# SSD steps of a hybrid backbone: the forward products of the masked C.B scores move from GpSimd to ScalarE

## What is computed

```
def step(h, inp):                       # one chunk of 128 tokens
    cum = jnp.cumsum(dtc * a, axis=1)
    seg = cum[:, :, None, :] - cum[:, None, :, :]
    decay = jnp.exp(jnp.where(lower[None, :, :, None], seg, -jnp.inf))
    xdt = xc * dtc[..., None]
    scores = jnp.einsum('blhn,bshn->blsh', cc, bc) * decay
    y = jnp.einsum('blsh,bshp->blhp', scores, xdt)
    ...
yx_f, _ = _ssd_scan(xx, dtx[:, :, 0], a[0], bx, cx, sc_f)
yx_b, _ = _ssd_scan(flip(xx), flip(dtx[:, :, 1]), a[1], flip(bx), flip(cx), sc_b)
```

## Time and profile before

| | us |
|---|---|
| median of 3 runs | 1758.17 (1756.37 to 1759.17) |
| the profiled execution's own time | 1754.64 |
| its span | 1753.4 |
| TensorE busy | 1565.6 (89%) |
| VectorE busy | 1120.2 (64%) |
| ScalarE busy | 733.8 (42%) |
| GpSimd busy | 303.9 (17%) |

### The profile page before, as it was taken

How to read it: one execution, slowest core, us unless ns; L and a number is a source line. 1 busy time by engine, 2 the same in 40 slices (tenths; PEclk the granted TensorE clock), 3 DMA queues, 4 the chain that set the end, 5 groups by cost and what they waited for, 6 DMA issues and landing times.

```text
span 1753.4 us, 22888 instructions
## 1 busy us (share of the span) xinstructions
PE 1565.6 (89%) x8633; PEld 1283.8 (73%) x8633; DVE 1120.2 (64%) x1694; ACT 733.8 (42%) x1291; POOL 303.9 (17%) x379
## 2 busy tenths in 40 slices
PE   5699999999976999988878999989999899998877
PEld 2577877777765789766556877767788788887766
DVE  0257888887777465655645645535336778888875
ACT  1435444544434334355453522322334445554442
POOL 0011433343333101100000000000001023322330
PEclk7589999999978999999989989989899899999888
DMA  9432455335440322222432143442441343343333
GB/s 287 136 91 81 121 144 160 112 113 151 139 144 24 108 96 79 82 73 73 144 121 84 49 147 111 151 144 73 144 138 38 88 130 99 100 116 97 99 106 108
DMA packets 169422, 197.40 MB, mean 113 GB/s; under 512 B 9696, under 2 KB 151648, under 8 KB 169312
## 3 DMA queue, kind: packets, MB, share of 16 engines
q1 hardware_dynamic: 158480, 163.08, 29.2%
q0 software_dynamic: 9296, 30.19, 6.8%
q10 hardware_dynamic: 1536, 2.67, 0.5%
HBM read 194.59 MB, written 1.31 MB: 112 GB/s over the span
## 4 chain that ended last, share of the span: by engine, by line
PE 53%; DVE 28%; ACT 8%; issue 8%; DMA 2%; ACTq 0%; POOL 0%; DVEq 0%
PE ps L400 14%; PE ps L401 13%; PE ps L402 13%; DVE xc L809 6%; DVE w_lo L369 4%; PE ps L424 3%; DVE cum_b L817 3%; PE ps L562 2%; PE ps L568 2%; DMA raw<-in_mod_w 2%; ACT Wb L714 2%; DVE Wb L836 2%; DVE Hs L851 1%; ACT w_hi L362 1%; PE ps L1624 1%
## 5 line engine op out<-in xcount | busy, mean ns | idle before, releaser
L400 PE MATMUL ps<-h_hi,w_hi 128*128 128x512 f32 (+1 forms) x1056 | 407.1, 386 | 14.5 <-DVE w_lo L369 14.0
L401 PE MATMUL ps<-h_lo,w_hi 128*128 128x512 f32 (+1 forms) x1056 | 393.7, 373 | 0.0
L402 PE MATMUL ps<-h_hi,w_lo 128*128 128x512 f32 (+1 forms) x1056 | 393.2, 372 | 0.0
L369 DVE TENSOR_TENSOR w_lo<-raw,w_hi 128x1024 fp32r<-128x1024 f32 (+1 forms) x205 | 244.4, 1226 | 148.9 <-ACT w_hi L362 147.3
L362 ACT ACTIVATE w_hi<-raw 128x1024 fp32r<-128x1024 f32 (+1 forms) x205 | 208.1, 1049 | 135.8 <-PE ps L402 126.6
L400 PEld LDWEIGHTS ps<-h_hi,w_hi 128*128 128x128 f32 x1056 | 202.9, 192 | 60.9 <-issue 26.1
L402 PEld LDWEIGHTS ps<-h_hi,w_lo 128*128 128x128 f32 x1056 | 202.3, 192 | 34.9
L401 PEld LDWEIGHTS ps<-h_lo,w_hi 128*128 128x128 f32 x1056 | 202.9, 192 | 32.5
L809 DVE SCALAR_TENSOR_TENSOR xc<-ps,gp,xc 128x508 f32<-128x508 f32 (+1 forms) x224 | 162.7, 728 | 41.8 <-ACT xc L683 35.8
L400 PE MATMUL ps<-w_hi,h_hi 128*128 128x512 f32 (+2 forms) x368 | 134.3, 365 | 21.1 <-DVE w_lo L369 18.4
L402 PE MATMUL ps<-w_hi,ylo 128*128 128x512 f32 x384 | 151.5, 395 | 0.0
(11 more groups left out here) (236 smaller groups left out, 2795.2 us busy)
## 6 DMA issues: line engine op xcount, KB each, us to landing
raw<-in_mod_w SPq DMA_DIRECT2D x96, 512.0 KB, 4.7
raw<-in_ssm_w_in SPq DMA_DIRECT2D x64, 512.0 KB, 5.1
cum_b<-cum_scratch POOLq DMA_DIRECT2D x96, 256.0 KB, 5.0
raw<-in_ssm_w_in SPq DMA_DIRECT2D x66, 256.0 KB, 3.9
raw<-in_ssm_w_out SPq DMA_DIRECT2D x32, 512.0 KB, 4.6
raw<-in_pool_w_in SPq DMA_DIRECT2D x32, 512.0 KB, 4.6
raw<-in_attn_w_in SPq DMA_DIRECT2D x20, 512.0 KB, 3.9
raw<-in_pool_w_out SPq DMA_DIRECT2D x16, 512.0 KB, 4.4
```

The source lines that it names most:

```text
L369: dve.tensor_tensor(lo[:, 0:width], raw[:, r % RS, 0:width], hi[:, 0:width].bitcast(F32), ALU.subtract).then_inc(lo_done, 1)
L400: pe.matmul(o, hi_s, hi_m, start=first, stop=False)
L401: pe.matmul(o, hi_s, lo_m, start=False, stop=False)
L402: return pe.matmul(o, lo_s, hi_m, start=False, stop=last)
```

## The change

GpSimd's `forward_part` goes, with its semaphore `wa_g` and the two waits of VectorE on it. `cb_dt(n)` on ScalarE makes both products: four activations for `Wa`, then four for `Wb`, with the step sizes of either direction as scale. Its waits stay as they are: the second mask of the step (`cbm_d`), and from chunk 2 on `m_d` of two chunks before. The activations read `cb[:, 0]` or `cb[:, 1]` and write as before; no other instruction changes.

```
@@ act: cb_dt(n)
-            for h in range(HG):
-                last = act.activation(Wb[:, n % 2, h, :], cb[:, 1, c, :], ACT.Copy,
-                                      scale=sg[:, g, 48 + 4 * c + h:49 + 4 * c + h])
+            for d, W in ((0, Wa), (1, Wb)):
+                for h in range(HG):
+                    o = 32 + 16 * d + 4 * c + h
+                    last = act.activation(W[:, n % 2, h, :], cb[:, d, c, :], ACT.Copy, scale=sg[:, g, o:o + 1])
             last.then_inc(s["cbdt_a"], 1)
@@ dve: masks()
             if g:
-                dve.wait_ge(s["wa_g"], nc * g)
                 dve.wait_ge(s["cbdt_a"], nc * g)
@@ dve: mix(n)
             dve.wait_ge(s["cbdt_a"], nc * g + n + 1)
-            dve.wait_ge(s["wa_g"], nc * g + n + 1)
@@ pool: ssd_pool_step
-        def forward_part(n):
-            c = first + n
-            pool.wait_ge(s["cbm_d"], 2 * g + 1)
-            if nc * g + n >= 2:
-                pool.wait_ge(s["w_d"], nc * g + n - 1)
-            pool.tensor_tensor(Wa[:, n % 2, :, :], cb[:, 0, c, :].unsqueeze(1).broadcast_to((128, HG, 128)),
-                               spread(sg[:, g, 32 + 4 * c:36 + 4 * c], 128), ALU.mult).then_inc(s["wa_g"], 1)
-
...
-        forward_part(0)
-        forward_part(1)
...
-        for n in range(2, nc):
-            forward_part(n)
```

## The result

The changed kernel took 1793.34 us (median of four runs, 1792.16 to 1797.75) beside 1758.67 us (1756.37 to 1759.85) of the kernel before: ratio 1.020, 95% interval 1.0187 to 1.0213. It is slower, 3 us above the forecast of 1790. The profiled execution has a span of 1791.0 us against 1753.4, 37.6 us more.

What follows compares the result with a forecast made beforehand. The prediction took the scan-step loop through ScalarE's products, the tap, VectorE and TensorE as the bound. Layer 0 +10.2, layer 3 +18.5 and clock +3 gave +31.7 us: 1790 us against 1758.17, range 1776 to 1806.

Steps and rivals of the forecast that it cites:

- What bounds: Scan steps: a loop of ScalarE's head products, tap, VectorE, TensorE and ScalarE again sets the step.
- Rival C: No change: ScalarE's added 60 us lie in its idle time, as its 42% busy suggests; 1755 to 1761 us, chance 0.03.
- rival B: Faster: VectorE's freed time decides and scan steps lose only the 0.85 us collision; 1750.6 us, chance 0.03.
- D: Clock recovers early: TensorE's longer gap brings 5 us or less at half speed in both layers; 1774 to 1783, chance 0.12.
- Part 1: Eight more activations at the scan step's head, ahead of the tap VectorE awaits: +2.4 us in 14 steps, +33.6 us.
- Part 2: Products of chunks 2 and 3 in layer 0 grow to eight activations: costed at nothing, margin 0.7 us.
- Part 3: VectorE's sum in mix(1) freed of GpSimd's collision: -0.85 us in eight layer 0 steps, -6.8 us; -0.7 in layer 3.
- neither brings anything: On GpSimd, y (L989) and the cum_b DMAs move up but still wait for others: no gain.
- Part 4: Longer TensorE gap before the scan, then half-speed clock for 5 to 8.2 us: -4.5 to +10.9 us, taken +3.
- The sum: Layer 0 +10.2, layer 3 +18.5, clock +3: together +31.7 us, forecast 1790 us against 1758.17.

Runs made afterwards that it cites:

- experiment 1: Changed kernel with the forward (Wa) products of chunks 0 and 1 back on GpSimd: 1753.5 us, ratio 0.997 to the kernel before.
- experiment 4: Changed kernel with first_tap(1), silu(0) and the split of z ahead of cb_dt(0) and cb_dt(1) on ScalarE: 1720.8 us, ratio 0.9776 to the kernel before.
- experiment 2: Changed kernel with the forward products of chunks 2 and 3 of layer 0 back on GpSimd: 1793.6 us, ratio 1.020 to the kernel before.
- experiment 6: Kernel before, with first_tap(1), silu(0) and z split ahead of ScalarE's head products, and forward products of chunks 2 and 3 moved to ScalarE: 1728.6 us, 0.983.
- experiment 7: The changed kernel measured again, unaltered, on one chip with the kernels beside it: 1791.3 us, ratio 1.0182 to the kernel before.
- experiment 8: Changed kernel plus 14 useless TensorE matmuls in the gap before the scan of every scan step: 1791.9 us, ratio 1.0189; expected about 1763 us.
- experiment 9: Layer 3, next x's high part before silu(3), in three kernels: experiment 8's 1777.6 us, the changed kernel 1795.2 us, experiment 4's 1711.4 us.
- experiment 5: Kernel before, forward products still on GpSimd, with first_tap(1), silu(0) and the split of z ahead of cb_dt(0) and cb_dt(1) on ScalarE: 1737.8 us, 0.9879.

## Why the prediction was right

The sign and the mechanism held, and the time came within 3 us. Of that closeness a part is luck, as the sum below shows. Point by point:

- **What bounds.** Right: the loop through ScalarE's head. Experiments 1 and 4 show it from both sides: without the additional products ahead of the tap 1753.5 us, and with all of them but behind the tap and the split 1720.8. Rival C (the shares) and rival B are out. So is D (the clock back within 5 us), by the half-speed stretches under part 4. ScalarE's busy time rose by 54.8 us, where about 60 were foreseen, and GpSimd's fell by 63.7 instead of 56.
- **Part 1, +2.4 us in 14 steps.** Right to a tenth: VectorE's wait in step 5 grew by 2.39 us, and the total from 35.8 to 70.4 us, foreseen about 69. In layer 3 the wait for this tap grew by 2.0 to 2.4 us a step. TensorE's wait for the mixed scores reached 69.0 us and not the 75 foreseen. The single steps scatter more than foreseen: those of layer 3 grew by 1.8 to 3.1 us (2.4 or more foreseen), 17.6 in seven against 16.8 for part 1 alone, and those of layer 0 by 1.3 to 3.0 (0.8 to 2.3 foreseen).
- **Part 2, nothing.** Right: L835 waited for ScalarE only twice, 2.2 us in all, in step 8 of layer 0 as foreseen there. In step 5 the products of chunk 3 end at 407.5 and VectorE adds them at 408.27, a margin of 0.8 us where 0.7 was foreseen.
- **Part 3, -0.85 us in eight steps.** The duration is right (0.69 us everywhere), its worth only partly. Taken back alone in the changed kernel (experiment 2) it is 0.3 to 0.5 us a step, since `mix(1)` is then hidden in part behind TensorE's slow first chunk. A part is mis-sized, too: "neither brings anything" overlooked that VectorE's list shifts against GpSimd's squares. Step 5 before, VectorE and then GpSimd:

```profile
374.31 1.22 DVE L817 TENSOR_TENSOR cum_b<-cum_b,sg 128x1024 f32<-128x1024 f32 x1
375.57 1.67 DVE L819 TENSOR_TENSOR cum_b<-cum_b 128x512 f32<-128x512 f32 x1
...
377.94 1.39 DVE L851 TENSOR_TENSOR Hs<-Hs,sg 128x512 f32<-128x512 f32 x1
...
374.33 2.35 POOL L1011 TENSOR_TENSOR hf<-hf 128x512 f32<-128x512 f32 x1 [4.54 <-ACT hf L729]
377.49 1.29 POOL L1011 TENSOR_TENSOR hf<-hf 128x512 f32<-128x512 f32 x1 [0.81 <-ACT hf L729]
```

  Before, the squares held up one decay instruction and one state product (1.67 and 1.39 us for 0.69 each, 1.68 us too much); after, two decay instructions (2.31 for 1.22 and 1.66 for 0.69, 2.06 us too much). Steps 2 to 7 of layer 0 show the same pairs; the difference is 0.38 to 0.40 us in five of them and 0.74 in step 6, 2.7 us in all, and step 1 has none. The Trainium skill, page "SBUF — State Buffer", section "Who interferes with whom", says that order of issue decides who of the two is blocked. The squares agree with it: before, L817 began 0.02 us ahead of the first square and took its 1.22 us while the square took 2.35; after, the square began 0.25 us ahead, and the decay took 2.31. The pair of experiment 6 does not: there VectorE's instruction began 0.06 us ahead and was the one held. What I should have drawn from the page is that VectorE's list shifted by 2.4 us and the squares by 2.1, and that this makes new pairs.
- **Part 4, the clock, -4.5 to +10.9, taken +3.** The half-speed stretch after TensorE resumed was bounded by 5 and 8.2 us. It was about 7 us in steps 1 to 6 of layer 3, and 6.0 to 8.8 us in steps 2 to 6 of layer 0, above the bound in two (8.8 in step 3, 8.3 in step 5); in four of the five the clock fell before the gap was over. Step 5, TensorE alone (stretch, length, busy and count, granted clock, DMA share, GB/s):

```profile
399.00:400.50 1.50, 0.00 (x0) 1.00 0.00 0
401.00:402.50 1.50, 0.00 (x0) 0.50 0.00 0
402.80:409.60 6.80, 6.80 (x36) 0.50 0.12 36
411.50:413.00 1.50, 1.50 (x8) 1.00 0.99 309
```

  The gap ends at 402.77, and the clock had fallen some 2 us before it.
  What they cost is within the bounds, by subtraction. Layer 0 lost 14.4 us in seven steps, of which 7 x 1.55 = 10.9 are parts 1 and 3 and 2.7 the squares, so 0.8 are left. In layer 3 the 17.6 leave 0.8 over part 1. The second profile of the changed kernel (experiment 7) has 1.3 us more in layer 0 and 1.5 less in layer 3, so neither 0.8 is clear of what executions differ by. Within both profiles the stretch shows directly: of steps 2 to 6 of layer 0, those with 10.2 us of low clock, the part in the gap included, take 56.8 to 57.2 us, those with 6.8 take 55.8 to 56.3. The reason given for a small cost in layer 3, that TensorE would otherwise wait for w_lo, is what experiments 8 and 9 show.
- **The sum.** The terms give 31.7 us and the span grew by 37.6. From mask to mask they give 10.9 + 16.8 and 3 for the clock, 30.7, and the trace 32.0: the squares were missing (+2.7) and the clock cost 1.6 instead of 3, which cancels a part of that. Outside, the terms have 1.1 us (step 8 of both layers) and the trace 5.6. That part, 4.5 us, is unexplained; 1.8 of it lie ahead of the first scan step. The medians grew less than the spans, by 34.7 us: the profiled execution before was 4.0 us faster than its kernel's median, that after 1.1. So against the trace the sum is 5.9 us low, and against the medians 3.

My expectation of experiment 8 was wrong by more than the forecast was: I priced a stretch of TensorE by its own length and not by what came next.

## What to carry to other kernels

An engine that is 42% busy can still have no room at one place of its list: price a move by what is issued behind the new work and who waits for that, then look for a place in the same list where the work is needed last. Here the move cost 35 us at one place and gained 18 at another a few instructions later. Where a gap, a slow clock and a late weight lie beside each other, removing one shows the next, and effects measured one at a time do not add.

## What was not expected of the hardware

- A VectorE instruction with two SBUF inputs was held through six GpSimd instructions in a row, 4.07 us for one of 0.69 (experiment 6), and 3.94 us in experiment 5; in experiment 4, with starts at nearly the same distance in time, it took 1.13.
- In the changed kernel TensorE's granted clock fell to 0.50 inside a gap of 3.9 us in one step and just after the end of an equal gap in another, and the low stretch, with the part in the gap, was 6.8 us in some steps and 10.2 in others that look alike. After gaps of 1.4 us in layer 3 of experiment 4 it stayed at 1.00; after gaps of 1.88 us in experiment 8 it fell for 3.4 us in four of six steps of layer 3. What tells these cases apart stays open.
